# Router logits from unscaled tokens, norms on partitions, and the first expert's tokens by a product on chip

## The reference, cut to what matters

```python
h = rmsnorm(x, norm2_g[1])             # x * rsqrt(mean(x*x) + eps) * g
logits = h @ router_w                  # (264, 8)
top_v, top_i = lax.top_k(logits, 2)
probs = softmax(top_v)
out = sum over e of gates[:, e] * swiglu(h, w1[e], w3[e], w2[e])
x = x + out
```

## Time and profile before

| | |
|---|---|
| median of 3 runs | 1564.08 us (1561.28 to 1564.29) |
| profiled execution | 1564.02 us |
| its span, first to last instruction | 1562.3 us |
| outside the span | 1.7 us |
| PE busy | 1512.6 us (97%) |
| DVE, ACT, POOL busy | 1257.3, 962.8, 66.0 us |
| mean granted TensorE clock | 0.978 of 2.4 GHz |

### The profile page before, as it was taken

One profiled execution on the slowest core, in us unless ns is written; L12 is line 12 of the kernel. 1 busy time (PEld: TensorE's weight loads), 2 busy tenths in 40 slices (PEclk: granted clock), 3 DMA queues, 4 the chain that ended last, 5 costly groups with the idle time before them and its releaser, 6 DMA issues.

```text
span 1562.3 us, 23082 instructions
## 1 busy us (share of the span) xinstructions
PE 1512.6 (97%) x8414; PEld 1306.4 (84%) x8414; DVE 1257.3 (80%) x1243; ACT 962.8 (62%) x810; POOL 66.0 (4%) x68
## 2 busy tenths in 40 slices
PE   6999899998999989999999999999999999999997
PEld 5999899998999868888888888888888888888884
DVE  5786766667686858888888889888889889889897
ACT  4446443344446357777776776777677777777774
POOL 3000100000000110000000000000000000000000
PEclk9998999999998889999999999999999999999999
DMA  9541555554441559999999999999999999999992
GB/s 291 188 136 54 197 190 195 180 188 135 153 131 41 197 208 372 380 361 376 375 351 378 378 350 378 377 356 377 369 364 371 369 371 356 377 382 338 388 392 98
DMA packets 215729, 447.98 MB, mean 287 GB/s; under 512 B 7528, under 2 KB 63264, under 8 KB 215416
## 3 DMA queue, kind: packets, MB, share of 16 engines
q1 hardware_dynamic: 208176, 421.59, 74.6%
q0 software_dynamic: 6368, 23.38, 4.0%
q10 hardware_dynamic: 1136, 2.36, 0.4%
HBM read 433.98 MB, written 13.39 MB: 286 GB/s over the span
## 4 chain that ended last, share of the span: by engine, by line
PE 94%; DVE 4%; issue 1%; ACT 1%; DMA 1%; SPq 0%; DVEq 0%; POOLq 0%
PE ps L1448 28%; PE ps L1449 27%; PE ps L1450 27%; PE ps L1498 2%; PE ps L1761 2%; PE ps L1578 1%; PE ps L1464 1%; DVE w_lo L817 1%; PE ps L1598 1%; PE ps L1692 1%; PE ps L1734 1%; PE ps L1587 0%; DVE hF L838 0%; DVE rstd L835 0%; PE ps L1517 0%
## 5 line engine op out<-in xcount | busy, mean ns | idle before, releaser
L817 DVE TENSOR_TENSOR w_lo<-raw,w_hi 128x2048 fp32r<-128x2048 f32 x401 | 911.8, 2289 | 178.0 <-ACT w_hi L521 170.0
L521 ACT ACTIVATE w_hi<-raw 128x2048 fp32r<-128x2048 f32 x401 | 763.2, 1918 | 243.4 <-PE ps L1450 241.8
L1448 PE MATMUL ps<-w_hi,xg 128*128 128x512 f32 x896 | 360.2, 402 | 2.1 <-ACT xg L726 2.1
L1449 PE MATMUL ps<-w_lo,xg 128*128 128x512 f32 x896 | 355.4, 397 | 0.0
L1450 PE MATMUL ps<-w_hi,xg 128*128 128x512 f32 x896 | 355.4, 397 | 0.0
L1448 PE MATMUL ps<-h_hi,w_hi 128*128 128x264 f32 x736 | 215.9, 293 | 17.1 <-DVE h_lo L844 15.1
L1450 PE MATMUL ps<-h_hi,w_lo 128*128 128x264 f32 x736 | 211.4, 287 | 0.0
L1449 PE MATMUL ps<-h_lo,w_hi 128*128 128x264 f32 x736 | 211.3, 287 | 0.0
L1448 PEld LDWEIGHTS ps<-w_hi,xg 128*128 128x128 f32 x896 | 169.0, 189 | 41.0 <-ACT xg L726 2.3
L1450 PEld LDWEIGHTS ps<-w_hi,xg 128*128 128x128 f32 x896 | 169.1, 189 | 40.5
L1449 PEld LDWEIGHTS ps<-w_lo,xg 128*128 128x128 f32 x896 | 169.2, 189 | 37.7
(11 more groups left out here) (280 smaller groups left out, 1399.9 us busy)
## 6 DMA issues: line engine op xcount, KB each, us to landing
raw<-in_moe_w_dram SPq DMA_DIRECT2D x336, 1024.0 KB, 6.6
raw<-in_ffn_w_dram SPq DMA_DIRECT2D x33, 1024.0 KB, 5.2
raw<-in_w_in_dram SPq DMA_DIRECT2D x24, 1024.0 KB, 5.9
raw<-in_w_out_dram SPq DMA_DIRECT2D x8, 1024.0 KB, 5.3
hstate<-in_state_hgrn_dram POOLq DMA_DIRECT2D x2, 2048.0 KB, 12.1
out_dram<-hstate POOLq DMA_DIRECT2D x2, 2048.0 KB, 9.2
y_rows<-y_f POOLq DMA_DIRECT2D x4, 512.0 KB, 4.6
y_pair<-y_rows POOLq DMA_DIRECT2D x2, 1024.0 KB, 10.5
```

The source lines that it names most:

```text
L521: act.activation(w_hi[:, s, :], raw[:, r, :], ACT.Copy).then_inc(hi_made, 1)
L817: dve.tensor_tensor(w_lo[:, s, :], raw[:, r, :], w_hi[:, s, :].bitcast(F32), ALU.subtract).then_inc(split, 1)
L1448: pe.matmul(out, l_hi, r_hi, start=start, stop=False)
L1449: pe.matmul(out, l_hi, r_lo, start=False, stop=False)
```

## The change

The second norm of layer 1 no longer stands between the output projection and the router.

1. In the output loop DVE multiplies each finished chunk by the gain alone into `hF`, without the token's scale, and PE adds the logits of chunk c-1 after output chunk c (`route`): router columns are stationary, tokens stream. The logits come out as 8 rows of 264 and are turned by three small transposes.
2. The new state of a sample is computed one chunk later, and that of the last sample in the middle of the router's work (`last_state`). Constants of the router move into the loop (`router_base`, at chunk 4).
3. ACT squares each chunk right behind its add, POOL adds the eight squares (`sum_squares`), PE sums over channels into one column per token tile, ACT takes the root and DVE the reciprocal. The scale is applied when ACT copies `h_tok`, and to the difference of the two best logits.
4. The tokens of the first expert are not gathered from HBM. `first_slots` multiplies `h_tok` by `pick` (24 products of 128 columns) straight into the banks from which `xg` is made. The gather of the first expert is still issued, but nothing reads its rows.
5. Of the twelve turns, four come before the position counts, four before `first_slots`, and four after it. The weights of unit EX+2 are split later, behind the turns on ACT and behind the router on DVE. The four small stores of states on POOL come ahead of the large one, and the waits for finished stores move to the end of the program or to ACT.

```diff
@@ POOL
+            def sum_squares():
+                pool.wait_ge(sq_ready, 3 * DC + 1)
+                for c in range(1, DC):
+                    pool.wait_ge(sq_ready, 3 * DC + c + 1)
+                    link(pool.tensor_tensor(sq_sum, sq[:, 0, :] if c == 1 else sq_sum, sq[:, c, :],
+                                            ALU.add))
+                pool.sem_inc(sq_summed, 1)
...
+                if l == DEPTH - 1:
+                    store_rows(l)
+                    sum_squares()
                 pool.wait_ge(st_new, NSAMPLE * HEADS * (l + 1))
@@ ACT
-            norm(3, lambda c: 16 + 8 * FF_STEPS + c + 1)
-            hi(EX_BASE + 2)
...
+            for c in range(DC):
+                act.wait_ge(x_sum, 16 + 8 * FF_STEPS + c + 1)
+                act.activation(sq[:, c, :], xT[:, c, :], ACT.Square).then_inc(sq_ready, 1)
+                if c in (2, 4):
+                    hi(EX_BASE + (c - 2) // 2)
+            act.wait_ge(ssq_done, 4)
+            act.activation(root_t[:, 0:2], ps[:, 0, 0:2], ACT.Sqrt, bias=eps, scale=1.0 / D
+                           ).then_inc(root_done, 1)
...
+                    act.activation(h_tok[0:rows, t, cols], ps[0:rows, TURN_BANK[n], :], ACT.Copy,
+                                   scale=rstd_t[0:rows, t:t + 1]).then_inc(ht_taken, 1)
...
+            act.wait_ge(rstd_known, 1)
+            for n in range(4):
+                take_turn(n)
+            act.wait_ge(margin_ready, 1)
+            act.activation(rt[:, 9, :, 0], rt[:, 8, :, 0], ACT.Exp).then_inc(margin_exp, 1)
+            act.wait_ge(fin_stored, 16 * DEPTH)
+            for n in range(4, X_EARLY):
+                take_turn(n)
+            hi(EX_BASE + 2)
...
                     gather_high(0, 0)
                     gather_high(0, 1)
+                    for n in range(X_EARLY, 2 * X_TURNS):
+                        take_turn(n)
@@ DVE
+            def router_base():
+                link(dve.memset(rt[:, :, :, :], 0.0))
+                link(dve.memset(small[:, 144:150], 1.0))
+                link(dve.memset(tok_row[:, :, :, :], 1.0))
+                for t in range(3):
+                    link(dve.tensor_scalar(tok_row[:, t, :, 0], tok_row[:, t, :, 1],
+                                           tok_ids[:, t:t + 1], None, ALU.mult))
+                link(dve.tensor_scalar(spare_row, tok_ids[:, 0:1], 2.0 * T, None, ALU.add))
+                dve.tensor_copy(slot_row[:, 0:1], spare_row).then_inc(rows_known, 1)
...
                     dve.tensor_tensor(xT[:, c, :], xT[:, c, :], ps[:, c % 4, 0:T], ALU.add
                                       ).then_inc(x_sum, 1)
-                    new_state(c)
+                    if l == DEPTH - 1:
+                        dve.wait_ge(x_sum, 16 + 8 * FF_STEPS + c + 1)
+                        dve.tensor_scalar(hF[:, c, :], xT[:, c, :], v(V_N2 + DC + c), None,
+                                          ALU.mult).then_inc(h_full, 1)
+                        if c == 4:
+                            router_base()
+                    if l < DEPTH - 1:
+                        new_state(c)
+                    elif c:
+                        new_state(c - 1)
+                    if l == DEPTH - 1 and c == DC - 1:
+                        return lambda: new_state(c)
...
-            norm(3, V_N2 + 8, split_it=False)
-            lo(EX_BASE + 2)
-            dve.wait_ge(st_stored, 16 * DEPTH)
-            dve.wait_ge(fin_stored, 16 * DEPTH)
-            dve.wait_ge(rows_stored, 16 * (1 + 4 * DEPTH))
             dve.wait_ge(logits_done, 1)
+            dve.tensor_copy(logit_rows, ps[0:EXPERTS, LOGIT_BANK, 0:T]).then_inc(logits_taken, 1)
+            dve.wait_ge(logits_turned, 1)
...
+            dve.wait_ge(root_done, 5)
+            link(dve.reciprocal(rstd_t[:, 0:2], root_t[:, 0:2]))
+            link(dve.reciprocal(rstd_t[0:NSAMPLE, 2:3], root_t[0:NSAMPLE, 2:3]))
+            dve.sem_inc(rstd_known, 1)
...
+            last_state()
             dve.wait_ge(pos_done, 1)
...
-            slot_tokens(0, first=True)
...
-            dve.wait_ge(ht_taken, 2 * X_TURNS)
-            link(dve.memset(ps[:, 3:5, :], 0.0))
+            lo(EX_BASE + 2)
...
                     gather_low(0, 0)
                     gather_low(0, 1)
+                    slot_tokens(0, first=True)
@@ PE
+            def route(c):
+                pe.wait_ge(h_full, 3 * DC + c + 1)
+                ins = pe.matmul(ps[0:EXPERTS, LOGIT_BANK, 0:T], rw[:, c, :], hF[:, c, :],
+                                start=(c == 0), stop=(c == DC - 1))
...
+                    if l == DEPTH - 1 and c:
+                        route(c - 1)
                     spread_value(c)
...
+            route(DC - 1)
+            pe.wait_ge(sq_summed, 1)
+            for t, t0, n in TOKEN_TILES:
+                ins = pe.matmul(ps[0:n, 0, t:t + 1], sq_sum[:, t0:t0 + n], ones[:, 0:1], start=True,
+                                stop=True)
+            ins.then_inc(ssq_done, 1)
+            pe.wait_ge(logits_taken, 1)
...
-            for n in range(X_TURNS):
+            for n in range(4):
                 turn_tokens(n)
             pe.wait_ge(chosen_ready, 1)
...
+            def first_slots():
+                pe.wait_ge(ht_taken, X_TURNS)
+                pe.wait_ge(pick_ready, 3)
+                for c in range(DC):
+                    for t, _, n in TOKEN_TILES:
+                        ins = pe.matmul(ps[:, 5 + c // 4, P * (c % 4):P * (c % 4) + P],
+                                        h_tok[0:n, t, c * P:(c + 1) * P], pick[0:n, t, :],
+                                        start=(t == 0), stop=(t == 2))
+                ins.then_inc(xg_turned, 1)
+            for n in range(4, X_EARLY):
+                turn_tokens(n)
+            first_slots()
+            pe.wait_ge(base_ready, 1)
             find_slots(0, 0)
-            for n in range(X_TURNS, 2 * X_TURNS):
+            pe.wait_ge(blocks_ready, 1)
+            for n in range(X_EARLY, 2 * X_TURNS):
                 turn_tokens(n)
-            pe.wait_ge(ht_taken, 2 * X_TURNS)
-            turn_slots(0)
...
                 for j in range(4):
+                    if isinstance(b, int) and j == 2:
+                        pe.wait_ge(ht_taken, 2 * X_TURNS)
                     up_half(EX_BASE + j, i, j // 2, j % 2)
```

More of the change, by code:

```diff
@@ L196, in trunk @@
         unused = small[:, 45:46]
+        rstd_t = small[:, 144:147]
+        root_t = small[:, 147:150]
+        sq_sum = rstd[:, 0, :]
+        logit_rows = rstd[0:EXPERTS, 1, :]
         tok_ids = small[:, 150:153]
@@ L419, in _, with store_rows @@
                            ).then_inc(rows_stored, 16)
[L421 to L428, removed]
+            def store_rows(l):
                 pool.wait_ge(fin_ready, l + 1)
@@ L497, in _ @@
                     expert_block(b)
+            pool.wait_ge(st_stored, 16 * DEPTH)
+            pool.wait_ge(fin_stored, 16 * DEPTH)
+            pool.wait_ge(rows_stored, 16 * (1 + 4 * DEPTH))
         @block.scalar
@@ L702, in _, with take_turn @@
             mixer(1)
-            norm(3, lambda c: 16 + 8 * FF_STEPS + c + 1)
-            hi(EX_BASE + 2)
[L706 to L710, removed]
+            have_table(ACT.Sqrt)
+            for c in range(DC):
[6 more added lines that the diff above has]
+                           ).then_inc(root_done, 1)
+            act.activation(root_t[0:NSAMPLE, 2:3], ps[0:NSAMPLE, 0, 2:3], ACT.Sqrt,
+                           bias=eps[0:NSAMPLE, :], scale=1.0 / D).then_inc(root_done, 1)
+            def take_turn(n):
                 t, half = n % 6 // 2, n % 2
                 rows = TOKEN_TILES[t][2]
+                cols = slice(512 * half, 512 * half + 512)
                 act.wait_ge(ht_turned, n + 1)
-                dst = (h_tok if n < X_TURNS else x_tok)[0:rows, t, 512 * half:512 * half + 512]
-                act.activation(dst, ps[0:rows, TURN_BANK[n], :], ACT.Copy
-                               ).then_inc(ht_taken, 1)
+                if n < X_TURNS:
+                    act.activation(h_tok[0:rows, t, cols], ps[0:rows, TURN_BANK[n], :], ACT.Copy,
+                                   scale=rstd_t[0:rows, t:t + 1]).then_inc(ht_taken, 1)
+                else:
+                    act.activation(x_tok[0:rows, t, cols], ps[0:rows, TURN_BANK[n], :], ACT.Copy
+                                   ).then_inc(ht_taken, 1)
                 if n < X_TURNS and half:
@@ L1684, in _ @@
             mixer(1, 2)
-            norm(3)
-            pe.wait_ge(rw_landed, 16)
-            for c in range(DC):
-                pe.wait_ge(h_full, 3 * DC + c + 1)
-                for t, t0, n in TOKEN_TILES:
-                    ins = pe.matmul(ps[0:n, LOGIT_BANK[t], 0:EXPERTS], hF[:, c, t0:t0 + n],
-                                    rw[:, c, :], start=(c == 0), stop=(c == DC - 1))
-            ins.then_inc(logits_done, 1)
+            route(DC - 1)
[5 more added lines that the diff above has]
+            pe.wait_ge(logits_taken, 1)
```

(4 more changed lines are left out.)

63 lines of the change are left out of this document (38 added, 25 removed).

## The result

The changed kernel takes 1555.76 us, the median of 11 runs; the kernel before, run beside it on the same chip, 1564.08. The ratio is 0.9946, 95% interval 0.9935 to 0.9957: faster by 0.54%, some 8.3 us. The forecast was 1552.7, so the direction and the size are as foretold, with a gain that is 3 us smaller. One of the eleven runs took 2534.25 us at a mean granted clock of 0.592; it is left out of the ratio, and without it the median is 1555.66. The profiled execution took 1560.95 us (span 1559.1, mean granted clock 0.978).

What follows compares the result with a forecast made beforehand. PE was taken to pace the expert stage, so starting it earlier ends the program earlier. Gain 12.2 less 0.5 and 0.4 is 11.3 us, against 1564.02 that is 1552.7; range 1547.4 to 1559.6.

Steps and rivals of the forecast that it cites:

- the 533.0 allowed: Norm beside the router: its sums may come until 533.0 at no cost, covered by the state of sample 6.
- signs of being wrong: Among the signs listed: POOL's adds over 1 us with PE waiting for the square sums; a 1.2 GHz clock beyond 548.
- the place that the prediction named: PE's wait for the sums, in front of the logits' turns; each us beyond the cover would be paid in full.
- The third and fourth rivals: Third: POOL's adds hold DVE, 4.2 us, 1556.4, chance 0.08. Fourth: adds wait until DVE pauses, 1569, chance 0.05.
- the 0.5 taken for contention: Output loop: POOL's seven adds may hold DVE, between 0 and 6.8 us; 0.5 us was taken.
- 14.0 in the sum: Expert stage start: `y_rows` cleared 14.0 us behind the product's end, behind the first gather on POOL.
- the 0.4 allowed: Clearing of `y_rows` before DVE's first results: a weight load in between would cost 0 to 0.6 us; 0.4 taken.
- the second rival: Expert stage start: clearing `y_rows` replaces the gather as the wait, 6.2 us late, 1558.5 us; chance 0.07.
- a cover of 2.0: Expert stage start: `y_rows` cleared at 14.0, DVE's first results needing it at 16.0 us behind the product's end.
- the lower level until 546.6: Product replacing the gather: five instructions at the lower clock, then 43 x 0.111 us at the higher, ending at 551.3.
- the first rival: The product runs at the lower clock until 556.7, first expert product at 561.3, time 1559.4 us; chance 0.12.
- the forecast's two costs: Subtracted from the gain of 12.2 us: 0.5 for POOL's adds holding DVE, 0.4 for the late clearing of `y_rows`.

Runs made afterwards that it cites:

- after: The changed kernel without further edit, its first profiled execution: 1560.95 us.
- after again: The changed kernel repeated without edit, third profile of it: median 1554.88 us, ratio 0.9939, profiled at 1555.26 us.
- the sixteen runs above: Runs of the unedited changed kernel at mean clock 0.978 or more: three take 1560.03 to 1561.78 us, the other thirteen 1553.66 to 1558.0.

## Why the prediction was right, and where it missed

Positions from `s_fin`, as predicted and in two of the profiles:

| | predicted | after (clock stays low) | after again (clock returns) |
|---|---|---|---|
| last scaled chunk | 531.7 - 495.3 = 36.4 | 531.35 - 493.89 = 37.5 | 37.5 |
| experts chosen | 538.8 - 495.3 = 43.5 | 537.96 - 493.89 = 44.1 | 44.1 |
| product starts | 545.4 - 495.3 = 50.1 | 544.02 - 493.89 = 50.1 | 49.7 |
| product ends | 551.3 - 495.3 = 56.0 | 558.71 - 493.89 = 64.8 | 57.9 |
| first expert product | 553.75 - 495.3 = 58.5 | 563.56 - 493.89 = 69.7 | 60.5 |

The position counts start where the experts are chosen. In the kernel before they start at 548.50 - 495.29 = 53.2, and its first expert product stands at 565.92 - 495.29 = 70.6, at full clock. So the changed loop and router bring 9.1 us in both outcomes. From there to the first expert product it was 17.4, and is 25.6 where the clock stays low and 16.4 where it returns; with padding it is 554.22 - 540.90 = 13.3. What the start gains passes to the end, give or take 1.5 us: from the first expert product to the last instruction it is 1562.3 - 565.92 = 996.4 before, and 995.5, 997.8 and 996.7 in the three profiles of the changed kernel.

**Right: output loop, router, positions.** The loop ended 1.1 later than worked out: DVE's last add waits 0.78 for PE, so PE's added logits set the end there, not DVE alone. The router made up half of that. The product starts where the forecast had it, to within half a us. This is the part of the gain that comes surely: with the gather in place of the product, and the store out of its way, the time is the same 1556. What the logits in the loop and the norm beside it bring, each alone, was not run.

**Right: the norm is free beside the chain.** The sums were ready at 532.54, half a us ahead of the 533.0 allowed and 0.9 ahead of PE's turns, though an add takes 0.75 to 1.03 and not 0.6. One of its signs of being wrong, adds over 1 us, did show (1.01 and 1.03), but the other half of it, PE waiting for the sums, did not. Doubled, they cost 0.85 at the place that the prediction named. The third and fourth rivals did not occur: in the changed kernel's loop DVE's instructions are as long as before (0.42 for the add, 2.28 for a low part), so the 0.5 taken for contention was too much. The Trainium skill, "GPSIMD Engine Reference", section "Key points", has POOL and VectorE share an SBUF interface; the doubled adds bear it out in kind, with low parts of 2.51 instead of 2.28 and one scaling of 0.89 instead of 0.36, on DVE's side. By its section "Elementwise — side-by-side cycle accounting" an add was an estimated 0.58; the measured ones are 30 to 80% above that.

**Right: what moves behind is covered.** `y_rows` was cleared 572.53 - 558.71 = 13.8 behind the product's end, 14.0 in the sum, and DVE's first results came at 577.14, 4.6 later; the 0.4 allowed was not needed, and the second rival did not occur. Where the clock returns, the late turns are shorter and the cover is smaller. In the third profile `y_rows` was cleared at 568.77 and DVE's first results came at 570.34: 1.6, where the sum had a cover of 2.0.

One thing that moved was not priced: the prediction has nothing on the chain waiting for the large store of states. That holds for the kernel as built, where the pick (1.60 beside that store) ends before the middle turns. With the gather back on the chain the store's place was worth 5.8.

**Mis-sized: the product.** The step took every one of the 48 instructions at the price of 128-row weights. Eight of 24 products have 8-row weights, and the pauses at both of their sides cost 2.9 us at 2.4 GHz and 3.5 at 1.2. With them the product is 8.24 instead of 5.9 even where the clock returns before it. That is 2.3 us, most of what the forecast was too fast by, and it leaves the first expert product 2.0 late in that outcome; padding, which removes the pauses, gave 1551.05.

**Half right: the clock.** The step "the lower level until 546.6" describes one of two outcomes, in which the return came even before the product. In the other, shown in two profiles, the clock does not come back until the product is over, which is the first rival, and the prediction's sign "a clock of 1.2 GHz beyond 548". The slot sums and late turns are as that rival has them (1.4 + 3.2, measured 1.37 and 3.48), and the pauses come on top. Its time, 1559.4, lies near the 1560.95 of after partly by luck: its first expert product is at 561.3 - 495.3 = 66.0 from `s_fin`, 3.7 before the measured 69.7, its sum leaves out the 0.9 of the forecast's two costs, and that execution reached `s_fin` 1.4 earlier than the kernel before. The rival had a chance of 0.12; three of the sixteen runs above look like it.

The forecast's reason for the return, that it came "about 4 us into the turns" in the kernel before, leaves out what the earlier trace rows show ahead of those turns: 8.74 us of logits, through which PE was busy as well, at the lower clock. So PE was "dense" in those rows from 534.93 on, and the clock was back only from about 547.8. A dense PE was no sure sign of a return, and that the median lies in the outcome which the forecast took is in part luck.

## What to carry to other kernels

Cost a matmul by the shape of its stationary tile, and where a short tile sits between full ones, pad it if the buffer has room. When a gather is replaced by on-chip products, list what ran under the gather: it now stands in front of or behind the products. A store that is moved to make room lands somewhere else; look at which transfer on the path waits with it.

## What the runs showed of the hardware

- Products with 8 rows between products with 128 rows leave a pause of 0.22 to 0.23 us on both sides at 1.2 GHz. With 128 rows in all of them, the 48 instructions take 5.36 instead of 8.24 us at 2.4 GHz.
- The granted clock stayed at 1.2 GHz through 14.69 us of a product that the profile shows as busy without a gap on PE; in another execution of the same program it was back at 2.4 GHz before that product, while PE made the middle turns.
- While POOL issued the 2 MB store, DVE's three pick instructions took 1.83 us instead of 0.68; the long one ended with the issue (545.18 and 545.16).
- A 32 KB store took 6.92 us beside that store, 1.77 without it; the gather after it took 5.28 and 4.31.
